# Output projection: weights and two tiles of mixed rows loaded and split inside the samples' recurrence

## The reference, cut to what matters

```python
def trunk_layer(x, w, past):
    h = rmsnorm(x, w['norm1_g'])
    proj = jnp.einsum('nld,dc->nlc', h, w['w_in'])
    ...
    oc, s_fin = rwkv_mixer(zc, z_before, s0, w)
    mix = jnp.concatenate([oa.reshape(N, L, A_Q), ob.reshape(N, L, B_W), oc], axis=-1).astype(x.dtype)
    x = x + jnp.einsum('nlc,cd->nld', mix, w['w_out'])
    u = jnp.einsum('nld,df->nlf', rmsnorm(x, w['norm2_g']), w['mlp_up'])
    x = x + jnp.einsum('nlf,fd->nld', jnp.square(jax.nn.relu(u)), w['mlp_down'])
```

## Time and profile before

| | us |
|---|---|
| median of 3 runs (3477.84 to 3482.94) | 3480.81 |
| the profiled execution | 3479.05 |
| its span, first to last instruction | 3477.0 |
| samples' recurrence, SP's first load to the end of the barrier | 1645.1 to 1744.9 |
| output projection, from SP's first load | 1744.9 |
| first matmul of the output projection | 1762.3 |

### The profile page before, as it was taken

How to read it: one execution, slowest core, us unless ns; L and a number is a source line. 1 busy time by engine, 2 the same in 40 slices (tenths; PEclk the granted TensorE clock), 3 DMA queues, 4 the chain that set the end, 5 groups by cost and what they waited for, 6 DMA issues and landing times. The chain is left out here.

```text
span 3477.0 us, 65868 instructions
## 1 busy us (share of the span) xinstructions
PE 3181.9 (92%) x27146; PEld 2683.6 (77%) x27146; DVE 1595.8 (46%) x3079; ACT 824.1 (24%) x1515; POOL 350.7 (10%) x473
## 2 busy tenths in 40 slices
PE   8999998998885889887679799999999999999998
PEld 7999996566564878776458578888887888888887
DVE  6111121776115666663234344444445544454445
ACT  5000000655002333321123222112112322221112
POOL 3000001642003332421000000000000000000000
PEclk9999999999667999998589899999999999999999
DMA  4221223520512001000055531111112410111111
GB/s 148 72 71 67 70 77 96 146 66 21 213 59 65 20 29 41 24 12 24 11 180 170 159 133 49 48 48 40 40 42 98 151 49 25 48 48 48 48 43 62
DMA packets 142820, 248.61 MB, mean 71 GB/s; under 512 B 21440, under 2 KB 101248, under 8 KB 139784
## 3 DMA queue, kind: packets, MB, share of 16 engines
q1 hardware_dynamic: 142600, 245.44, 21.1%
HBM read 184.88 MB, written 60.52 MB: 71 GB/s over the span
## 5 line engine op out<-in xcount | busy, mean ns | idle before, releaser
L2539 DVE TENSOR_TENSOR m_y<-m_y,m_db 128x512 f32<-128x512 f32 x512 | 351.8, 688 | 324.7 <-PE m_db L2308 324.3
L2306 PE MATMUL m_ub<-m_hh,m_wuh 128*128 128x352 f32 (+1 forms) x1280 | 452.2, 353 | 19.8 <-DVE m_hl L2485 19.8
L2307 PE MATMUL m_ub<-m_hl,m_wuh 128*128 128x352 f32 (+1 forms) x1280 | 450.5, 352 | 0.0
L2308 PE MATMUL m_ub<-m_hh,m_wul 128*128 128x352 f32 (+1 forms) x1280 | 450.1, 352 | 0.0
L2306 PE MATMUL m_db<-m_wdh,m_uh 128*128 128x512 f32 x1024 | 407.4, 398 | 4.8 <-DVE m_wdl L2494 4.7
L2308 PE MATMUL m_db<-m_wdh,m_ul 128*128 128x512 f32 x1024 | 404.3, 395 | 0.0
L2307 PE MATMUL m_db<-m_wdl,m_uh 128*128 128x512 f32 x1024 | 403.4, 394 | 0.0
L186 PE MATMUL p_bank<-p_xh,p_wh 128*128 128x416 f32 x800 | 286.6, 358 | 11.9 <-DVE p_wl L307 11.9
L187 PE MATMUL p_bank<-p_xl,p_wh 128*128 128x416 f32 x800 | 284.0, 355 | 0.0
L188 PE MATMUL p_bank<-p_xh,p_wl 128*128 128x416 f32 x800 | 283.1, 354 | 0.0
L2306 PEld LDWEIGHTS m_ub<-m_hh,m_wuh 128*128 128x128 f32 x1280 | 241.4, 189 | 48.3 <-issue 13.5
(11 more groups left out here) (401 smaller groups left out, 5270.8 us busy)
## 6 DMA issues: line engine op xcount, KB each, us to landing
m_wur<-w_up SPq DMA_DIRECT2D x64, 512.0 KB, 6.1
m_wdr<-w_dn SPq DMA_DIRECT2D x64, 512.0 KB, 4.3
out_projT<-p_ob SPq DMA_DIRECT2D x100, 208.0 KB, 1.9
cp_z<-out_projT SPq DMA_DIRECT2D x8, 1408.0 KB, 6.8
p_kc<-kbT SPq DMA_DIRECT2D x8, 1344.0 KB, 5.9
p_vc<-vb SPq DMA_DIRECT2D x8, 1344.0 KB, 8.7
p_wr<-w_fm SPq DMA_DIRECT2D x20, 512.0 KB, 3.7
p_mix<-mixT SPq DMA_DIRECT2D x16, 512.0 KB, 5.0
```

The source lines that it names most:

```text
L2306: pe.matmul(out, wh, mh, start=first, stop=False)
L2307: pe.matmul(out, wh, ml, start=False, stop=False)
L2308: return pe.matmul(out, wl, mh, start=False, stop=last)
L2539: dve.tensor_tensor(yh, yh, db[(2 * a + h) % ND][:, :], ALU.add).then_inc(y_added, 1)
```

## The change

A new class `OutWeights` holds the projection's weight tiles, the two buffers of mixed rows with their split parts, and their semaphores. It is created around the samples' recurrence and lives on through `out_project`. The raw weights `wr` are freed when the recurrence ends. Three of its methods are called in `rwkv` for the samples: SP issues eight loads of weights (512 KB each, each with its own semaphore) and two of mixed rows right after the constants; ACT makes high copies in `prepare` at i = 6 to 9, two k blocks each time, with the mixed rows' after blocks 0 and 1; DVE makes all the low parts in `special`, between `vm` and `um`. In `out_project` what did this is gone, and PE waits once for all eight low parts. The two tiles of mixed rows are columns 0 to 255, which the prompt's stages have written and stored. No arithmetic changes.

```diff
@@ rwkv, scalar_walk, prepare
+                if i in (6, 7, 8, 9) and ahead and not isinstance(e, Rehearsal):
+                    for k in (2 * i - 12, 2 * i - 11):
+                        ahead.high(e, k)
@@ rwkv, vector_walk, special
                     V.done(i, name, 0)
+                    if name == "vm" and ahead and not isinstance(e, Rehearsal):
+                        for k in range(KC):
+                            ahead.low(e, k)
@@ rwkv, sync
             for dst, src_ in consts:
                 sp.dma_start(dst, src_).then_inc(c_in, 16)
+            if ahead:
+                ahead.load(sp)
@@ class OutWeights
+    def load(self, sp):
+        for k in range(KC):
+            sp.dma_start(self.wr[:, k, :], self.w_o[:, k, :]).then_inc(self.w_in[k], 16)
+        for t in range(2):
+            sp.dma_start(self.m[t][:, :, :], self.mixT[:, :, P * t:P * (t + 1)].rearrange("k p n -> p k n")).then_inc(self.mix_in[t], 16)
+    def high(self, act, k):
+        act.wait_ge(self.w_in[k], 16)
+        act.activation(self.wh[:, k, :], self.wr[:, k, :], ACT.Copy).then_inc(self.w_high, 1)
+        if k < 2:
+            act.wait_ge(self.mix_in[k], 16)
+            act.activation(self.mh[k][:, :, :], self.m[k][:, :, :], ACT.Copy).then_inc(self.m_high, 1)
+    def low(self, dve, k):
+        dve.wait_ge(self.w_high, k + 1)
+        dve.tensor_tensor(self.wl[:, k, :], self.wr[:, k, :], self.wh[:, k, :].bitcast(F32), ALU.subtract).then_inc(self.w_low, 1)
+        if k < 2:
+            dve.wait_ge(self.m_high, k + 1)
+            dve.tensor_tensor(self.ml[k][:, :, :], self.m[k][:, :, :], self.mh[k][:, :, :].bitcast(F32),
+                               ALU.subtract).then_inc(self.m_low, 1)
@@ out_project, sync
-            load_mix(0)
-            for i in range(WP):
-                sp.dma_start(wr[i][:, :, :], w_o[:, i * KC // WP:(i + 1) * KC // WP, :]).then_inc(w_in[i], 16)
-            load_mix(1)
             load_x(0)
@@ out_project, tensor
+            pe.wait_ge(w_low, KC)
             for t, (r0, n) in enumerate(tiles):
...
-                        if t == 0 and h == 0 and k % (KC // WP) == 0:
-                            pe.wait_ge(w_low, k * WP // KC + 1)
@@ out_project, scalar
-            high_m(0)
-            for i in range(WP):
-                act.wait_ge(w_in[i], 16)
-                act.activation(wh[:, i * KC // WP:(i + 1) * KC // WP, :], wr[i][:, :, :], ACT.Copy).then_inc(w_high, 1)
-            high_m(1)
@@ out_project, vector
-            low_m(0)
-            for i in range(WP):
-                dve.wait_ge(w_high, i + 1)
-                ks = slice(i * KC // WP, (i + 1) * KC // WP)
-                dve.tensor_tensor(wl[:, ks, :], wr[i][:, :, :], wh[:, ks, :].bitcast(F32), ALU.subtract).then_inc(w_low, 1)
-            low_m(1)
```

More of the change, by code:

```diff
@@ L1184, in __getattr__, with rwkv @@
         return lambda *a, **k: self
-def rwkv(nc, outer, tag, sample, src, shift0, state0, cst, wts, mixT, col0, state_out):
+def rwkv(nc, outer, tag, sample, src, shift0, state0, cst, wts, mixT, col0, state_out, ahead=None):
     nb, nq = (NB, NQ) if sample else (1, 256)
@@ L1945, in rwkv_constants, with __init__, staging, out_project @@
     return out
-def out_project(nc, outer, mixT, xtok, w_o, g2, ident, x2, h2T):
+class OutWeights:
+    def __init__(self, nc, ctx, outer, mixT, w_o):
+        s = Scope(nc, ctx, outer)
+        self.wh = s.sb("p5_wh", [P, KC, D], F32R)
+        self.wl = s.sb("p5_wl", [P, KC, D], F32R)
+        self.m = [s.sb(f"p5_mix{i}", [P, KC, P]) for i in range(2)]
+        self.mh = [s.sb(f"p5_mh{i}", [P, KC, P], F32R) for i in range(2)]
+        self.ml = [s.sb(f"p5_ml{i}", [P, KC, P], F32R) for i in range(2)]
+        self.w_in = [s.sem(f"p5_w_in{i}") for i in range(KC)]
+        self.w_high = s.sem("p5_w_high")
+        self.w_low = s.sem("p5_w_low")
+        self.mix_in = [s.sem(f"p5_mix_in{i}") for i in range(2)]
+        self.m_high = s.sem("p5_m_high")
+        self.m_low = s.sem("p5_m_low")
+        self.mixT, self.w_o = mixT, w_o
+    def staging(self, nc, ctx, outer):
+        self.wr = Scope(nc, ctx, outer).sb("p5_wr", [P, KC, D])
+    def load(self, sp):
[16 more added lines that the diff above has]
+                               ALU.subtract).then_inc(self.m_low, 1)
+def out_project(nc, outer, ahead, mixT, xtok, g2, ident, x2, h2T):
     NT = SEQ // P + 1
@@ L1953, in out_project @@
         s = Scope(nc, ctx, outer)
[L1954 to L1957, removed]
+        wh, wl, m, mh, ml = ahead.wh, ahead.wl, ahead.m, ahead.mh, ahead.ml
+        w_low, mix_in, m_high, m_low = ahead.w_low, ahead.mix_in, ahead.m_high, ahead.m_low
         g = s.sb("p5_g", [P, KC])
@@ L1960, in out_project @@
         eps = s.sb("p5_eps", [P, 1])
-        m = [s.sb(f"p5_mix{i}", [P, KC, P]) for i in range(2)]
-        mh = [s.sb(f"p5_mh{i}", [P, KC, P], F32R) for i in range(2)]
-        ml = [s.sb(f"p5_ml{i}", [P, KC, P], F32R) for i in range(2)]
         xt = [s.sb(f"p5_x{i}", [P, D]) for i in range(2)]
@@ L1972, in out_project @@
         eps_set = s.sem("p5_eps_set")
[L1973 to L1976, removed]
         x_in = [s.sem(f"p5_x_in{i}") for i in range(2)]
-        m_high = s.sem("p5_m_high")
-        m_low = s.sem("p5_m_low")
         producted = s.sem("p5_producted")
@@ L2610, in decoder_trunk @@
         rwkv(nc, outer, "cp", False, zc, None, None, cst, wts, mixC, 0, A["state_p"])
-        rwkv(nc, outer, "cs", True, zc, A["shift0"], A["state0"], cst, wts, mixC, SEQ, A["state_s"])
-        out_project(nc, outer, mixT, A["x"], A["w_o"], A["g2"], A["cst_ident"], x2, h2T)
+        with ExitStack() as kept:
+            ahead = OutWeights(nc, kept, outer, mixT, A["w_o"])
+            with ExitStack() as raw:
+                ahead.staging(nc, raw, outer)
+                rwkv(nc, outer, "cs", True, zc, A["shift0"], A["state0"], cst, wts, mixC, SEQ, A["state_s"], ahead=ahead)
+            out_project(nc, outer, ahead, mixT, A["x"], A["g2"], A["cst_ident"], x2, h2T)
         mlp(nc, outer, h2T, x2, A["w_up"], A["w_dn"], A["fg"], A["cst_sel"], A["y"])
```

## The result

The changed kernel takes **3458.92 us** (median of 5 runs, 3452.16 to 3466.17) against 3482.01 (5 runs, 3477.84 to 3482.94): ratio 0.9937, 95% interval 0.9921 to 0.9953. By the ratio that is 22 us less; the two medians lie 23.1 apart. It is faster, as forecast, but by more: the forecast was 3465.4, and the lower end of the range, 3461, lies above the result. The profiled execution took 3452.16 us (span 3450.1) and the one before 3479.05 (span 3477.0), 26.9 us more.

What follows compares the result with a forecast made beforehand. PE was taken as the limit, except while it stood still at the output projection's opening. The sum -17.3 + 0.3 + 1.6 = -15.4 us on 3480.81 gave a median of 3465.4, range 3461 to 3471.

Steps and rivals of the forecast that it cites:

- What bounds the kernel: Output projection's opening: PE idle from 1745.0 to 1762.2 us; time taken from in front of 1762.3 comes off the end.
- PE's start: Behind the projection's barrier: PE starts 0.3 us after 1745.0 instead of at 1762.31, so -17.3 + 0.3 us.
- The copies on ACT: Samples' recurrence, in front of `cs_tok`: ten copies take 9.7 us against 8.08 idle, so `cs_tok` starts 1.6 us late.
- The loads: Samples' recurrence: ten early loads land before ACT asks for them; cost 0, with 1.9 us as upper end.
- both rivals about loads: Samples' recurrence: loads hold the constants back, 3472.6 to 3479.7 us, 8%; or each pays whole latency, 3487.8 us, 3%.
- The subtractions: DVE between `vm` and `um` in the samples' recurrence: ten take 12.2 us at most, 3.4 of cover left; cost 0.
- Clock: PE's first projection matmuls: clock stays at 0.50 for 4.8 us after the first, as now; about 12 slow ones; 0.
- The clock rivals: Projection's tile 0 or MLP's start: clock stays low or rises later, 3472.6 us, 8%; or rises earlier, 3459 to 3463, 6%.
- an earlier rise of the clock: PE's clock rises sooner in the projection's tile 0 or at the MLP's start, giving 3459 to 3463 us; chance 6%.
- Late next is PE itself: Projection behind the barrier: additions, `x` and tile 2 come in time, so PE's own pace limits, 0.231 us a fast matmul.
- The range: Whole kernel: 3461 to 3471 us, holding the forecast's about 3462 to 3470 (74%) and part of the clock's cases.

## Why the prediction was right and wrong

- **What bounds the kernel**: right. The time in which PE stood still behind the barrier came off the end.
- **PE's start**: right. Lag 0.20 us, forecast 0.3.
- **The copies on ACT**: right in mechanism and nearly in size. They took 9.48 us, forecast 9.7, and `cs_tok` was 1.3 late in place of 1.6. The Trainium skill's figures (ScalarE: Activation LUTs, "What ACT_TABLE_LOAD costs") had given an estimate of 9.55, the nearer one: the overlap of two copies was 1.04 - 0.95 = 0.09 us. A third of my error came from 1.05 for one copy, the rest from the two ends: the first copy began 0.10 us before the square root's end, and `cs_tok` 0.09 before the last copy's.
- **The loads**: right. ACT waited for none, and DVE's first instruction came 12.8 us behind the stage's first load, where it was 13.0 before, so that both rivals about loads fell. SP stood for most of the 6.48 us at its two issues of mixed rows, which cost nothing, since it had nothing else to do. The Trainium skill's rule for the most bandwidth, at least 1 MiB in a DMA (DMA: Bandwidth & Descriptors, "Rules for kernel authors"), had nothing to win here: eight loads of 512 KB, hidden, cost PE nothing. No run here tries larger ones.
- **The subtractions**: right. 4.12 us of DVE's cover were left, forecast 3.4.
- **Clock**: near. 14 slow matmuls in 5.97 us, forecast about 12; DVE's first addition came 0.2 us later after PE's start than before. The clock rivals did not decide this. That the time lies at the edge of the 3459 to 3463 that the prediction gave to an earlier rise of the clock (6%) is chance: there was no earlier rise.
- **"Late next is PE itself", at an unchanged pace: wrong.** This is the step that failed, a term missing from the sum. I took 0.231 us a matmul for everything behind the barrier, since the diff touches no instruction there. The diff does touch where the operands lie. That was worth 4.3 us in the trace, and 5.0 in the medians (ratio 0.9986, interval 2 to 8 us) when done alone. With the old layout the kernel comes to 15.9 us less.
- **The MLP's start: a second missing term**, 1.65 us. In the eleven traces with the early loads PE begins it in 7.2 to 7.8 us, in the three without in 8.5 to 9.0; it is the landing of the first weights, 3.59 us against 5.25. Why an earlier load of other weights should speed this one is open.
- **The range** had only known unknowns in it, most of them losses. Its upper end was added up wrong too: 3469.9 with 2.5 us of spread is 3472.4, not 3470. With the two terms in the sum, -15.4 - 4.3 - 1.7 = -21.4, the forecast would have been 3459.4, against 3458.92. So close a match is partly luck: the five runs lie 14 us apart.

## What to carry to other kernels

Work that stands behind a barrier only because its code is written there can be begun in an earlier stage; here the early loads, with the splitting cut into blocks behind the barrier, already brought 13.7 of 17.2 us. The splitting is to be put where its engine waits with more room than the work takes. When a diff moves tiles, cost the move as a part of its own, and try it alone: here a fifth of the gain came from three small tiles that no longer lay in front of the matmul's stationary operand. Reserving small constants last cost nothing where it was tried; whether it brings something has to be measured stage by stage, since it did little in the input projection.

## What the runs showed of the hardware

The start of a matmul's stationary tile within SBUF changed its pace. For 128x512 matmuls on fp32r tiles of 128x128, back to back at 2.4 GHz in the output projection, the spacing was 0.2273 us with the tiles at multiples of 256 bytes, as their sizes give it (256, 512, 4096 seen), and 0.2334 behind 548 bytes of constants, 2.7% more. A tile of rows took 11.78 us in the one case and 12.08 in the other; 64 bytes above a multiple took 12.08 as well, 128 above 12.02. At the two places tried for the streamed operand it made no difference. In the input projection (416 columns) such a move was worth 0.1893 against 0.1884 to 0.1887 us, and in the MLP nothing (0.232), which leaves the conditions open. The second surprise is the prompt's recurrence, which lasted 593.1 to 605.4 us with the same instructions, more than most edits here are worth: at a granted clock of 0.94 in the shortest and 0.91 in the longest. So a term of 1 us is read here from its stretch of the trace, not from the total.
